# Splitting the first weight unit by k-tile, and moving two later splits of a unit, in a two-layer transformer kernel on one core

## The chip, the core and the metric

The kernel runs on one core of a Trainium2 chip. The metric is the time on the device in microseconds (us) of one execution. Engines are named as in the profile: PE multiplies matrices, PEld loads its stationary operands, ACT is the scalar engine, DVE the vector engine, POOL the GpSimd engine, and SP only issues transfers (DMAs). Each runs its own list of instructions in order and waits on semaphores.

## The reference

Two layers over 256 tokens of 1024 features, all in float32. Layer 0 is NSA attention (16 heads, 4 key/value heads; a compressed, a selected and a window branch, gated), layer 1 is MoBA attention. Behind each attention come a residual with layer norm, a SwiGLU network of width 2816, and again a residual with layer norm.

```python
for i in range(DEPTH):                       # DEPTH = 2
    a = nsa_mixer(x, ...) if i % 2 == 0 else moba_mixer(x, ...)
    x = layer_norm(ALPHA * x + a, ln1_g[i], ln1_b[i])
    f = (jax.nn.silu(x @ wg) * (x @ wu)) @ wd
    x = layer_norm(ALPHA * x + f, ln2_g[i], ln2_b[i])
```

With 256 tokens both attentions see every block, so what is left is causal attention, plus the compressed branch in layer 0.

## The kernel before, in words

**Products.** Each float32 operand is kept as two fp32r parts, hi (rounded by ACT, `copy`, L418) and lo (the rest, subtracted by DVE, `minus`, L685). One float32 product is three matmuls: hi by hi, lo by hi, hi by lo (L1036 to L1038). The 256 tokens are two halves of 128 rows.

**Units.** All weights stream from HBM as 96 units of 128 x 2048 floats (1 MB), each four k-tiles of 128 x 512. Units go round three buffers `raw` and four buffers `w_hi`, `w_lo`. SP loads unit u + 3 when the rest of unit u is taken (`lo_ready`); ACT rounds unit u when it has landed and PE has finished unit u - 4 (`w_used`, in `round_unit`); DVE subtracts (`rest_of_unit`); PE multiplies (`one_unit`, `rows_by_weights`): for each token half four k-tiles of three matmuls, 24 in all. `round_to(n)` on ACT and `rest_to(n)` on DVE do all units below n that are not yet done; where these calls stand in ACT's and DVE's lists is written by hand.

**Opening.** x (transposed) comes in four quarters of 256 KB: for each token half, k-tiles 0 to 3 and 4 to 7, in the order (half 0, first), (half 1, first), (half 0, second), (half 1, second). Units 0 and 1 come in the pieces of `PIECES`: unit 0 as k-tiles 0, 1, and 2 with 3; unit 1 as two pairs. ACT's queue loads the first two pieces, SP's queue the rest and x. ACT rounds and DVE subtracts in the order x0, piece 0, x1, piece 1, piece 2, x2, piece 3, x3, piece 4. PE first runs 25 products of a constant tile (`WARM_UP`, 256 columns, bf16, their result is not used) and then takes each piece for both token halves.

**NSA attention.** Sixteen jobs of two heads each. PE: scores of job i + 2, turn the probabilities of job i, weigh the values of job i - 1 (L1214, L1229, L1247). DVE: `row_maxima(i + 2)`, `scale_probs(i + 1)`. ACT: exp(i + 2). Unit 11, used by PE after job 14, is subtracted by DVE in four quarters, `rest_of_quarter`, in jobs 1 to 4.

**Chunk end.** A SwiGLU network is eleven chunks of 256 hidden features; c = 10 is the last. PE turns the hidden rows (L1313), ACT rounds them (`hidden_hi`, tile last_hi), DVE subtracts (`hidden_lo`, last_lo), PE makes the last down products, and DVE adds the residual (L915), takes the statistics (L920) and writes x (L942), which PE turns (L1071) for the next layer. In the first network unit 48 (the second of layer 1) is rounded whole behind last_hi and subtracted whole behind last_lo.

Of the kernel before, what the change touches and what calls it, by code (L numbers as in the profile page):

```python
# [26 lines left out]
HALF = 2  # L27
# [32 lines left out]
def build(nc, x_rows, x_cols, stream, w_gates, w1, w2, cpos, positions, norms, out):  # L60
# [8 lines left out]
    with ExitStack() as ctx:  # L69
# [84 lines left out]
        piece_in = [sem(f"piece_in{n}") for n in range(3)]  # L154
# [102 lines left out]
        PIECES = (((0, 1), (1, 2), (2, 4)), ((0, 2), (2, 4)))  # L257
# [4 lines left out]
        def open_piece(u, n):  # L262

            return 2 * u + n
# [39 lines left out]
        def _(sp):  # L304
# [9 lines left out]
            load_x(0)  # L314
            load_x(1)
            load_piece(0, 2)
            load_x(2)
            load_piece(1, 0)
            load_x(3)
            load_piece(1, 1)  # L320
# [93 lines left out]
        def _(act):  # L414
# [11 lines left out]

            def round_to(end):
                for u in range(units[0], end):
                    round_unit(u)
                units[0] = max(units[0], end)  # L430
# [36 lines left out]
            part_hi(0, 0)  # L467
            x_hi(1)
            part_hi(0, 1)
            part_hi(0, 2)  # L470
            x_hi(2)
            part_hi(1, 0)
            x_hi(3)
            part_hi(1, 1)
# [118 lines left out]
            def ffn(u0, c0):  # L593
# [36 lines left out]
                silu_of(c, u0 + 3 * c + 1)  # L630
                hidden_hi(c, last_hi)
                round_to(min(UNITS, u0 + 3 * c + 5))
# [36 lines left out]
        def _(dve):  # L669
# [21 lines left out]
            def rest_of_quarter(u, n):  # L691
                at = slice(512 * n, 512 * (n + 1))
                if n == 0:
                    dve.wait_ge(hi_ready, u + 1)
                ins = minus(w_lo[:, u % SLOTS, at], raw[:, u % RAW, at], w_hi[:, u % SLOTS, at].bitcast(f32))
                if n == 3:
# [45 lines left out]
            part_lo(0, 0)  # L742
            x_lo(1)
            part_lo(0, 1)
            part_lo(0, 2)
            x_lo(2)
            part_lo(1, 0)
            x_lo(3)
            part_lo(1, 1)
# [97 lines left out]
            def attend(jobs, job, j0, a0, u):  # L847
# [33 lines left out]
                row_maxima(0)  # L881
                row_maxima(1)
                scale_probs(0)
                scale_probs(1)
                if j0 > 0:
                    rest_to(u + 2)
                for i in range(jobs):
# [4 lines left out]
                    if j0 == 0 and 1 <= i <= 4:  # L892
                        rest_of_quarter(u + 1, i - 1)
# [77 lines left out]
            def ffn(u0, c0):  # L971
# [36 lines left out]
                hidden(c)  # L1008
                hidden_lo(c, last_hi, last_lo)
                rest_to(min(UNITS, u0 + 3 * c + 5))  # L1010
# [22 lines left out]
        def _(pe):  # L1033
# [82 lines left out]
            for _ in range(WARM_UP):  # L1116
                nc.tensor.matmul(ps[:, 7, 0:256], warm_in[:, 0:P], warm_in[:, :], start=True, stop=True)
            for u in range(2):
                for n, (k0, k1) in enumerate(PIECES[u]):
                    if last_piece(u, n):  # L1120
                        pe.wait_ge(lo_ready, u + 1)
                    else:
# [368 lines left out]
```

## Time and profile before

| | us |
|---|---|
| median of 3 runs | 659.43 (659.05 to 659.87) |
| profiled execution | 659.21 |
| its span, first to last instruction | 657.5 |
| PE busy | 641.8 (98%) |
| PEld busy | 512.7 (78%) |
| DVE busy | 399.8 (61%) |
| ACT busy | 313.1 (48%) |
| DMA traffic | 113.03 MB, mean 172 GB/s |

The span is shorter than the time by 1.7 us, which lie around the program. Busy times overlap; an engine's busy time counts for the end only where the others wait for it. A matmul's row is longer than its share of PE's time, since the next one starts before it has drained: the distance from start to start is the cost. The same holds in part for ACT and DVE.

### The profile page before, as it was taken

How to read it: one execution, taken by the hardware profiler on the slowest of the kernel's cores; microseconds unless marked ns; L12 is line 12 of the kernel's file. 1: busy time of each engine (PE TensorE's matmuls, PEld its weight loads, DVE VectorE, ACT ScalarE, POOL GpSimd, SP SyncE). 2: the span in 40 equal slices, each digit the busy share in tenths (PEclk: the TensorE clock that was granted, in tenths of full speed). 3: DMA queues.
4: the chain of work that ended last, by engine and by line, in shares of the span. 5: the costliest groups of instructions: out<-in, count | busy, mean ns of one | idle time of the engine just before them, and what ended most of it. 6: DMA issues, size and time to landing. Idle time of an engine off the chain costs nothing.

```text
span 657.5 us, 8484 instructions
## 1 busy us (share of the span) xinstructions
PE 641.8 (98%) x3265; PEld 512.7 (78%) x3265; DVE 399.8 (61%) x506; ACT 313.1 (48%) x438; POOL 16.3 (2%) x56
## 2 busy tenths in 40 slices
PE   7999999999999999999999999999999999999995
PEld 5887766677888888888867887778788888888874
DVE  4694679868565554444467755786675555544437
ACT  4664578935453444444433645793353344444420
POOL 2000000000000000000000000000100000000001
PEclk8999999999999999999999999999999999999999
DMA  8984311035574555555542654303656555555301
GB/s 299 360 334 183 129 65 65 2 129 191 169 285 187 191 193 191 191 189 179 183 151 94 250 177 173 140 29 125 232 199 253 189 190 191 191 191 191 128 1 64
DMA packets 18574, 113.03 MB, mean 172 GB/s; under 512 B 2800, under 2 KB 3312, under 8 KB 5872
## 3 DMA queue, kind: packets, MB, share of 16 engines
q1 hardware_dynamic: 16384, 102.65, 42.9%
q10 hardware_dynamic: 1008, 5.77, 2.3%
q0 software_dynamic: 1152, 4.19, 1.9%
q8 instruction: 21, 0.34, 0.2%
q14 instruction: 9, 0.07, 0.0%
HBM read 111.56 MB, written 1.05 MB: 171 GB/s over the span
## 4 chain that ended last, share of the span: by engine, by line
PE 86%; DVE 10%; ACT 2%; DMA 1%; issue 1%; DVEq 0%; SPq 0%; ACTq 0%
PE ps L1036 25%; PE ps L1038 24%; PE ps L1037 24%; PE ps L1214 2%; DVE w_lo L685 2%; PE ps L1247 2%; PE ps L1313 2%; PE ps L1229 1%; DVE bn L920 1%; DVE x L934 1%; DVE x L915 1%; PE ps L1155 1%; DMA twice<-x_cols 1%; DVE arena L869 1%; PE ps L1218 1%; ACT w_hi L418 1%
## 5 line engine op out<-in xcount | busy, mean ns | idle before, releaser
L685 DVE TENSOR_TENSOR w_lo<-raw,w_hi 128x2048 fp32r<-128x2048 f32 (+2 forms) x102 | 220.4, 2165 | 102.2 <-ACT w_hi L418 101.8
L1036 PE MATMUL ps<-w_hi,a_hi 128*128 128x512 f32 x592 | 235.8, 398 | 2.3 <-DVE a_lo L685 1.5
L1038 PE MATMUL ps<-w_hi,a_lo 128*128 128x512 f32 x592 | 231.4, 391 | 0.0
L1037 PE MATMUL ps<-w_lo,a_hi 128*128 128x512 f32 x592 | 231.1, 390 | 0.0
L418 ACT ACTIVATE w_hi<-raw 128x2048 fp32r<-128x2048 f32 (+2 forms) x99 | 184.2, 1863 | 96.6 <-PE ps L1038 88.7
L1036 PEld LDWEIGHTS ps<-w_hi,a_hi 128*128 128x128 f32 x592 | 111.6, 188 | 26.7 <-DVE a_lo L685 2.0
L1038 PEld LDWEIGHTS ps<-w_hi,a_lo 128*128 128x128 f32 x592 | 111.4, 188 | 24.0
L1037 PEld LDWEIGHTS ps<-w_lo,a_hi 128*128 128x128 f32 x592 | 111.7, 189 | 21.9
L1036 PE MATMUL ps<-w_hi,h_hi 128*128 128x512 f32 x160 | 62.4, 390 | 0.0
L1038 PE MATMUL ps<-w_hi,h_lo 128*128 128x512 f32 x160 | 62.3, 390 | 0.0
L1037 PE MATMUL ps<-w_lo,h_hi 128*128 128x512 f32 x160 | 62.2, 389 | 0.0
L597 ACT ACTIVATE arena<-ps 128x512 f32<-128x512 f32 x18 | 10.8, 598 | 68.4 <-PE ps L1038 68.4
L418 ACT ACTIVATE h_hi<-ps 128x512 fp32r<-128x512 f32 x20 | 12.0, 599 | 60.2 <-PE ps L1313 60.2
L551 ACT ACTIVATE arena<-ps,neg_max 128x128 f32<-128x128 f32 (+1 forms) x96 | 39.4, 446 | 2.3 <-DVE neg_max L853 2.3
L974 DVE TENSOR_TENSOR arena<-arena,ps 128x512 f32<-128x512 f32 x18 | 12.4, 688 | 37.9 <-ACT arena L597 37.9
L1038 PEld LDWEIGHTS ps<-w_hi,h_lo 128*128 128x128 f32 x160 | 30.0, 188 | 6.3
L1037 PEld LDWEIGHTS ps<-w_lo,h_hi 128*128 128x128 f32 x160 | 30.0, 188 | 6.2
L1036 PEld LDWEIGHTS ps<-w_hi,h_hi 128*128 128x128 f32 x160 | 30.0, 188 | 6.2
L418 ACT ACTIVATE arena<-ps 128x768 f32<-128x768 f32 (+2 forms) x28 | 23.5, 843 | 22.0 <-PE ps L1038 12.0
L685 DVE TENSOR_TENSOR h_lo<-ps,h_hi 128x512 fp32r<-128x512 f32 x20 | 13.8, 690 | 28.5 <-ACT h_hi L418 28.5
L853 DVE TENSOR_REDUCE neg_max<-ps 128x2 f32<-128x256 f32 (+1 forms) x48 | 24.4, 551 | 8.8 <-PE ps L1218 8.2
L418 ACT ACTIVATE a_hi<-ps 128x256 fp32r<-128x256 f32 (+1 forms) x28 | 13.7, 498 | 20.9 <-PE ps L1071 19.0
(150 smaller groups left out, 471.6 us busy)
## 6 DMA issues: line engine op xcount, KB each, us to landing
raw<-stream SPq DMA_DIRECT2D x94, 1024.0 KB, 4.8
arena<-w ACTq DMA_DIRECT2D x4, 1024.0 KB, 13.4
rows<-norms POOLq DMA_DIRECT2D x8, 512.0 KB, 4.6
raw<-stream SPq DMA_DIRECT2D x3, 512.0 KB, 9.1
twice<-x_cols SPq DMA_DIRECT2D x4, 256.0 KB, 7.6
x<-x_rows ACTq DMA_DIRECT2D x1, 1024.0 KB, 4.8
out<-x SPq DMA_DIRECT2D x3, 256.0 KB, 2.1
raw<-stream ACTq DMA_DIRECT2D x2, 256.0 KB, 5.9
```

Of the source, the lines that this page charges most:

```text
L418: return nc.scalar.activation(dst, src, ACT.Copy, scale=scale)
L551: last = nc.scalar.activation(probs[:, b, at:at + keys], ps[:, s_bank(b, h), P * half:P * half + keys], ACT.Exp, bias=neg_max[:, j0 + i, h ...
L597: nc.scalar.activation(silu[:, :, :], ps[:, 0:2, 0:FC], ACT.Silu).then_inc(silu_ready, 1)
L685: return nc.vector.tensor_tensor(dst, a, b, ALU.subtract)
L853: last = nc.vector.tensor_reduce(neg_max[:, j0 + i, half, :], ps[:, s_bank(b, 0):s_bank(b, 1) + 1, P * half:P * half + keys], AX.X, ALU.ma ...
L974: nc.vector.tensor_tensor(h_rows[:, :, :], silu[:, :, :], ps[:, 0:2, FC:2 * FC], ALU.mult).then_inc(h_ready, 1)
L1036: nc.tensor.matmul(dst, hi, m_hi, start=start, stop=False)
L1037: nc.tensor.matmul(dst, hi, m_lo, start=False, stop=False)
L1038: return nc.tensor.matmul(dst, lo, m_hi, start=False, stop=stop)
L1214: nc.tensor.matmul(ps[:, s_bank(b, h), P * half:P * half + keys], qT[on, q, P * half:P * (half + 1)], kk[on, k, 0:keys], start=half == 0, ...
L1247: nc.tensor.matmul(dst[HD * h:HD * (h + 1)], values[:, 0, cols[h]:cols[h] + HD], probsT[:, b, S * h:S * (h + 1)], start=j0 > 0, stop=False)
L1313: last = nc.tensor.transpose(hT_ps[:, half, t, :], h_rows[:, half, P * t:P * (t + 1)], ident[:, :])
```

## The change

The first unit now comes in four pieces of one k-tile (all 256 KB), and pieces 2 and 3 go ahead of the second x quarter, in SP's queue and in ACT's and DVE's order; unit 1's second piece goes ahead of the last x quarter. PE takes both units half by half: all pieces for token half 0, then for half 1, and between the pieces of unit 0's first half it runs four constant products each time (`BETWEEN`, twelve in all). In the NSA attention `rest_of_quarter` goes, and unit 11 is subtracted whole between `row_maxima(0)` and `row_maxima(1)`. At the end of the first network unit 48 is rounded and subtracted in two halves of 1024 columns, the first before last_hi and last_lo, the second behind them; the second network's end has no further unit and stays.

```diff
--- before.py
+++ after.py
@@ -151,7 +151,7 @@
         lo_ready = sem("lo_ready")
         w_used = sem("w_used")
         xT_in = [sem(f"xT_in{q}") for q in range(4)]
-        piece_in = [sem(f"piece_in{n}") for n in range(3)]
+        piece_in = [sem(f"piece_in{n}") for n in range(4)]
         piece_hi = sem("piece_hi")
         piece_lo = sem("piece_lo")
         warm_in_ready = sem("warm_in_ready")
@@ -254,14 +254,15 @@
 
         TURN_BANK = [(4, 5, 6, 7), (0, 1, 4, 5)] * 2
 
-        PIECES = (((0, 1), (1, 2), (2, 4)), ((0, 2), (2, 4)))
+        PIECES = (((0, 1), (1, 2), (2, 3), (3, 4)), ((0, 2), (2, 4)))
+        BETWEEN = 4
         WARM_UP = 25
 
         OUT_PIECES = ((0, 0, 512), (0, 512, 1024), (1, 0, 512), (1, 512, 768), (1, 768, 1024))
 
         def open_piece(u, n):
 
-            return 2 * u + n
+            return 3 * u + n
 
         def last_piece(u, n):
             return n == len(PIECES[u]) - 1
@@ -312,12 +313,13 @@
                 sp.dma_start(raw[:, u, at], stream[u, :, at]).then_inc(landed, 16)
 
             load_x(0)
+            load_piece(0, 2)
+            load_piece(0, 3)
             load_x(1)
-            load_piece(0, 2)
             load_x(2)
             load_piece(1, 0)
+            load_piece(1, 1)
             load_x(3)
-            load_piece(1, 1)
             sp.dma_start(raw[:, 2, :], stream[2]).then_inc(raw_in[2], 16)
             sp.dma_start(pos_i[:, :], positions).then_inc(small_in, 16)
             sp.dma_start(wg_raw[:, :, :], w_gates).then_inc(small_in, 16)
@@ -424,6 +426,15 @@
                     act.wait_ge(w_used, TURN_UNITS * later + (u - SLOTS + 1))
                 copy(w_hi[:, u % SLOTS, :], raw[:, u % RAW, :]).then_inc(hi_ready, 1)
 
+            def round_half_unit(u, part):
+                at = slice(1024 * part, 1024 * (part + 1))
+                if part == 0:
+                    act.wait_ge(raw_in[u % RAW], 16 * (u // RAW + 1))
+                    act.wait_ge(w_used, u - SLOTS + 1)
+                copy(w_hi[:, u % SLOTS, at], raw[:, u % RAW, at]).then_inc(piece_hi if part == 0 else hi_ready, 1)
+                if part == 1:
+                    units[0] = u + 1
+
             def round_to(end):
                 for u in range(units[0], end):
                     round_unit(u)
@@ -464,14 +475,13 @@
                 copy(w_hi[:, u, at], raw[:, u, at]).then_inc(hi_ready if last_piece(u, n) else piece_hi, 1)
 
             x_hi(0)
-            part_hi(0, 0)
+            for n in range(4):
+                part_hi(0, n)
             x_hi(1)
-            part_hi(0, 1)
-            part_hi(0, 2)
             x_hi(2)
             part_hi(1, 0)
+            part_hi(1, 1)
             x_hi(3)
-            part_hi(1, 1)
             units[0] = 2
             round_to(4)
             act.wait_ge(angles_ready, 1)
@@ -628,8 +638,11 @@
                 c = NFC - 1
                 round_to(min(UNITS, u0 + 3 * c + 4))
                 silu_of(c, u0 + 3 * c + 1)
+                if u0 < U_FF1:
+                    round_half_unit(u0 + 3 * c + 4, 0)
                 hidden_hi(c, last_hi)
-                round_to(min(UNITS, u0 + 3 * c + 5))
+                if u0 < U_FF1:
+                    round_half_unit(u0 + 3 * c + 4, 1)
 
             def nsa_values():
                 act.wait_ge(w_used, U_WO0)
@@ -688,12 +701,14 @@
                 dve.wait_ge(hi_ready, TURN_UNITS * later + (u + 1))
                 minus(w_lo[:, u % SLOTS, :], raw[:, u % RAW, :], w_hi[:, u % SLOTS, :].bitcast(f32)).then_inc(lo_ready, 1)
 
-            def rest_of_quarter(u, n):
-                at = slice(512 * n, 512 * (n + 1))
-                if n == 0:
+            def rest_of_half_unit(u, part, done):
+                at = slice(1024 * part, 1024 * (part + 1))
+                if part == 0:
+                    dve.wait_ge(piece_hi, 4 + done)
+                else:
                     dve.wait_ge(hi_ready, u + 1)
                 ins = minus(w_lo[:, u % SLOTS, at], raw[:, u % RAW, at], w_hi[:, u % SLOTS, at].bitcast(f32))
-                if n == 3:
+                if part == 1:
                     ins.then_inc(lo_ready, 1)
                     units[0] = u + 1
 
@@ -739,14 +754,13 @@
 
             nc.vector.memset(warm_in[:, :], 1.0).then_inc(warm_in_ready, 1)
             x_lo(0)
-            part_lo(0, 0)
+            for n in range(4):
+                part_lo(0, n)
             x_lo(1)
-            part_lo(0, 1)
-            part_lo(0, 2)
             x_lo(2)
             part_lo(1, 0)
+            part_lo(1, 1)
             x_lo(3)
-            part_lo(1, 1)
             units[0] = 2
             rest_to(3)
 
@@ -879,18 +893,17 @@
                     minus(a_lo[:, :, t, :], out_ps(t), a_hi[:, :, t, :].bitcast(f32)).then_inc(a_lo_ready, 1)
 
                 row_maxima(0)
+                if j0 == 0:
+                    rest_to(u + 2)
                 row_maxima(1)
                 scale_probs(0)
                 scale_probs(1)
-                if j0 > 0:
-                    rest_to(u + 2)
+                rest_to(u + 2)
                 for i in range(jobs):
                     if i + 2 < jobs:
                         row_maxima(i + 2)
                     if 0 < i and i + 1 < jobs:
                         scale_probs(i + 1)
-                    if j0 == 0 and 1 <= i <= 4:
-                        rest_of_quarter(u + 1, i - 1)
                     if i >= 2 and job(i - 2)[4]:
                         outputs_lo(i - 2)
                     if i >= jobs - 2:
@@ -1006,8 +1019,11 @@
                 c = NFC - 1
                 rest_to(min(UNITS, u0 + 3 * c + 4))
                 hidden(c)
+                if u0 < U_FF1:
+                    rest_of_half_unit(u0 + 3 * c + 4, 0, 1)
                 hidden_lo(c, last_hi, last_lo)
-                rest_to(min(UNITS, u0 + 3 * c + 5))
+                if u0 < U_FF1:
+                    rest_of_half_unit(u0 + 3 * c + 4, 1, 1)
 
             attend(**NSA)
             norm(0, U_FF0, A_O0)
@@ -1113,16 +1129,23 @@
 
 
             pe.wait_ge(warm_in_ready, 1)
-            for _ in range(WARM_UP):
-                nc.tensor.matmul(ps[:, 7, 0:256], warm_in[:, 0:P], warm_in[:, :], start=True, stop=True)
+            def constant_products(count):
+                for _ in range(count):
+                    nc.tensor.matmul(ps[:, 7, 0:256], warm_in[:, 0:P], warm_in[:, :], start=True, stop=True)
+
+            constant_products(WARM_UP)
             for u in range(2):
-                for n, (k0, k1) in enumerate(PIECES[u]):
-                    if last_piece(u, n):
-                        pe.wait_ge(lo_ready, u + 1)
-                    else:
-                        pe.wait_ge(piece_lo, open_piece(u, n) + 1)
-                    for half in range(HALF):
-                        pe.wait_ge(a_lo_ready, 2 * u + half + 1)
+                for half in range(HALF):
+                    for n, (k0, k1) in enumerate(PIECES[u]):
+                        if half == 0:
+                            if u == 0 and n > 0:
+                                constant_products(BETWEEN)
+                            if last_piece(u, n):
+                                pe.wait_ge(lo_ready, u + 1)
+                            else:
+                                pe.wait_ge(piece_lo, open_piece(u, n) + 1)
+                        if n == 0:
+                            pe.wait_ge(a_lo_ready, 2 * u + half + 1)
                         last = rows_by_weights(u, u, half, half, tiles=range(k0, k1))
                 last.then_inc(w_used, 1)
             chunk(2, (2, 3))
```

## Rows read from the trace of the kernel before

**Rows 1.** The page, chain that ended last: share of the span by engine.

```profile
PE 86%; DVE 10%; ACT 2%; DMA 1%; issue 1%; DVEq 0%; SPq 0%; ACTq 0%
```

**Rows 2.** Timeline of PE, 0 to 34 us: start us, us, what, [idle before <-releaser].

```profile
1.27 5.07 PE L1117 MATMUL ps<-warm_in 128*128 128x256 bf16 x25 [1.27 <-DVE warm_in L740]
7.00 0.50 PE L1036 MATMUL ps<-w_hi,a_hi 128*128 128x512 f32 x1 [0.66 <-DVE w_lo L685]
...
9.49 0.80 PE L1036 MATMUL ps<-w_hi,a_hi 128*128 128x512 f32 x1 [1.53 <-DVE a_lo L685]
...
12.62 0.39 PE L1037 MATMUL ps<-w_lo,a_hi 128*128 128x512 f32 x1
...
21.28 0.39 PE L1036 MATMUL ps<-w_hi,a_hi 128*128 128x512 f32 x1
```

**Rows 3.** Stretches: length, busy PE PEld DVE ACT POOL (starts), PEclk, DMA share, GB/s.

```profile
5.80:9.20 3.40, 1.51 (x8) 0.72 (x6) 1.59 (x3) 1.44 (x3) 0.00 (x0) 1.00 0.96 327
9.20:12.60 3.40, 3.11 (x7) 2.49 (x8) 2.41 (x4) 2.37 (x4) 0.00 (x0) 0.50 1.03 420
21.30:82.50 61.20, 61.20 (x363) 48.87 (x361) 41.13 (x59) 35.83 (x35) 1.25 (x2) 1.00 0.64 242
340.00:343.40 3.40, 2.04 (x10) 1.35 (x8) 3.19 (x7) 1.92 (x1) 1.00 (x1) 1.00 0.69 284
```

**Rows 4.** Timeline of ACT, 0 to 34 us.

```profile
8.73 0.63 ACT L418 ACTIVATE w_hi<-raw 128x512 fp32r<-128x512 f32 x1
...
11.97 1.06 ACT L418 ACTIVATE w_hi<-raw 128x1024 fp32r<-128x1024 f32 x1 [0.41 <-DMA raw<-stream]
...
16.44 1.92 ACT L418 ACTIVATE w_hi<-raw 128x2048 fp32r<-128x2048 f32 x1 [1.50 <-DMA raw<-stream]
```

**Rows 5.** Timeline of DVE, 0 to 34 us.

```profile
13.06 1.23 DVE L685 TENSOR_TENSOR w_lo<-raw,w_hi 128x1024 fp32r<-128x1024 f32 x1 [0.16 <-ACT w_hi L418]
```

**Rows 6.** DMA issues, 1.7 to 2.2 us (ACT's second piece): KB, us to landing.

```profile
raw<-stream ACTq DMA_DIRECT2D x1, 256.0 KB, 7.4
```

**Rows 7.** Timeline of DVE, 68 to 108 us.

```profile
85.88 1.02 DVE L853 TENSOR_REDUCE neg_max<-ps 128x2 f32<-128x256 f32 x2 [2.17 <-PE ps L1218]
...
94.25 0.68 DVE L685 TENSOR_TENSOR w_lo<-raw,w_hi 128x512 fp32r<-128x512 f32 x1
```

**Rows 8.** Timeline of PE, 86 to 118 us.

```profile
92.89 0.93 PE L1214 MATMUL ps<-kk,qT 64*128 64x128 f32 x8 [0.40 <-ACT arena L551]
...
94.39 0.66 PE L1229 MATMUL ps<-ident,arena 128*128 128x128 f32 x4 [0.25 <-DVE arena L869]
...
105.46 0.93 PE L1214 MATMUL ps<-kk,qT 64*128 64x128 f32 x8
...
106.54 0.60 PE L1229 MATMUL ps<-ident,arena 128*128 128x128 f32 x4
...
117.00 0.93 PE L1214 MATMUL ps<-kk,qT 64*128 64x128 f32 x8
```

**Rows 9.** Timeline of DVE, 322 to 362 us.

```profile
332.13 0.69 DVE L974 TENSOR_TENSOR arena<-arena,ps 128x512 f32<-128x512 f32 x1 [1.77 <-ACT arena L597]
334.20 0.69 DVE L685 TENSOR_TENSOR last_lo<-ps,last_hi 128x512 fp32r<-128x512 f32 x1 [1.38 <-ACT last_hi L418]
336.00 2.29 DVE L685 TENSOR_TENSOR w_lo<-raw,w_hi 128x2048 fp32r<-128x2048 f32 x1 [1.11 <-ACT w_hi L418]
...
342.79 1.41 DVE L942 SCALAR_TENSOR_TENSOR x<-x,rstd,rows 128x512 f32<-128x512 f32 x2
```

**Rows 10.** Timeline of PE, 322 to 362 us.

```profile
334.95 0.50 PE L1036 MATMUL ps<-w_hi,last_hi 128*128 128x512 f32 x1
...
343.60 1.32 PE L1071 MATMUL ps<-ident,x 128*128 128x128 f32 x8 [1.55 <-DVE x L942]
```

**Rows 11.** Timeline of DVE, 638 to 652 us.

```profile
647.47 1.41 DVE L942 SCALAR_TENSOR_TENSOR x<-x,rstd,rows 128x512 f32<-128x512 f32 x2
```

**Rows 12.** Timeline of PE, 638 to 652 us.

```profile
641.11 0.50 PE L1036 MATMUL ps<-w_hi,last_hi 128*128 128x512 f32 x1
```

## The prediction

> **What bounds the kernel now.** I read the chain of waits on the page first [rows 1]: 86% of it is PE, 10% DVE. So PE's queue of products sets the time, and only the places count where PE stands, or where its clock is low. Next came PE's own waits and its time in stretches. From 21.3 to 82.5 us PE is busy for all of 61.20 us [rows 3]; a shift of the work before passes through this stretch whole, whether it is a gain or a loss. The three places that the change touches are places where PE does not run full.
>
> 1. The opening. Twenty-five constant products run first, three real ones start at 7.00, the fourth at 9.49 after 1.53 us of standing for the second token part; from 9.49 on PE is dense [rows 2]. But the granted clock is 0.50 (1.2 GHz) from 9.2 to 12.6, after a stretch with 1.51 of 3.40 us busy [rows 3]. Seven products take 9.49 to 12.62, 0.45 us each; the 38 after them take 12.62 to 21.28, 0.228 each. At 21.28 unit 2 begins.
> 2. The first half of the NSA attention (jobs 2 to 6), where DVE's turn is longer than PE's.
> 3. The end of the first feed-forward network, where PE stands 1.55 us at 343.60 for x [rows 10].
>
> **The change part by part.**
>
> *Opening, the arrival of the pieces.* The queues carry the same bytes. Unit 0's half of 512 KB becomes two of 256 KB, and both are moved ahead of the second x quarter on SP's queue. That is one DMA more on SP (about 0.45 us of issue), with unit 2 and the six small loads behind it. The second piece (k-tile 1) was issued by ACT at about 1.3 and took 7.4 us, so it landed at 8.7 [rows 6]; ACT rounded it at 8.73 [rows 4]. Before, PE did not need it at 9.49: it went on with the same k-tile for the other token half. Now it is the next thing needed: ACT to 9.35, DVE 0.68 us, PE at 10.07. That is 0.58 us later than 9.49. The pieces behind it follow at ACT's 0.6 us, so DVE ends them at 10.65 and 11.2, and x quarter 1 at 11.85. Unit 1's first piece was rounded before x quarter 3 and stays at 14.2 (the 1024 form starts at 13.06 and gives way at 14.20 [rows 5]); its second piece is now before x quarter 3 and ends near 15.4, the quarter at 16.2, early enough for the last twelve products.
>
> *Opening, PE's sum.* From 10.07 there are 45 products, as before from 9.49, and eight constant products among them (the first four of the twelve lie in the standing time). A constant product took 0.20 us on average (25 in 5.07) [rows 2]; it has half the columns of a real one, so at the full clock I take 0.11. With the clock high the whole time: 10.07 + 45 x 0.228 + 8 x 0.11 = 21.2. Unit 2 cannot start before its rest is there: it lands at 16.44, then 1.92 of ACT and 2.29 of DVE make 20.7 [rows 4, 9]; that bound is not the later one. So unit 2 starts at 21.2 instead of 21.28: a gain of 0.1 us, with 0.6 as the most. If the constant products cost 0.20 each, it is a loss of 0.6. If the clock falls at 9.2 and rises at 12.6 as before, 2.5 us run at half pace, which costs 1.25 us more: a loss of 1.15. I take the gain of 0.1, because constant products now stand behind the first piece, but this is the weakest step.
>
> For this the Trainium skill has a sentence (TensorE: Matmul & The Clock Gate, Part 1): the same kernel can show a different count of slow products from run to run, because the points at which the gate is set don't follow the kernel's start. One profile cannot test it. By it, the opening's term would wander between the two values above from run to run, and the median would lie between them.
>
> The trace shows both sides of the clock question: 1.51 of 3.40 us busy was followed by the low clock, while 2.04 of 3.40 us at 340.0 to 343.4 was not [rows 3]. The four constant products behind the first piece bring the first figure to about 2.1 (0.11 x 4 and a tail of 0.17), like the second, though the second has dense work before it.
>
> *Cutting finer.* DVE takes 0.68 us for 512 columns and gives way to the next after 0.60; for 1024 it is 1.23 and 1.14 [rows 5, 7]. So an added cut costs 0.06 us of DVE. That is beside other work in the opening, where PE does not wait for DVE after 10.07, and the quarters that go from the attention were four at 0.60.
>
> The Trainium skill (VectorE: DVE Perf Modes, the errata section) says that an instruction that reads SBUF pays a fixed latency of its own, exposed between instructions, and gives (N + 151)/0.96 ns for a tensor_tensor. The durations agree (0.69 and 1.22 by it), the distance between starts doesn't: by the page four quarters would cost 2.76 us and their removal up to 0.36 more, where the row shows 2.4.
>
> *Unit 11 in the attention.* Removed: four quarter subtractions, 0.60 of pitch each, in jobs 1 to 4. Added: one whole subtraction (2.29, pitch 2.19) between the first two row maxima. DVE stands 2.17 us there, until 85.88, for the scores of job 1 [rows 7]; the whole unit runs 83.63 to 85.82 in that gap, so its cost is nothing with 0.05 to spare, and were the cover gone, the full 2.2 would shift exp(1) and job 2. What goes? PE starts the scores of job 4 at 92.89 and those of job 8 at 105.46: 12.57 us. The next four jobs, where PE is never late, take to 117.00: 11.54 [rows 8]. The excess is 1.03. Of it, 0.42 lies at 94.39, 1.50 after the scores began where 106.54 is 1.08 after 105.46; that turn waits for job 2's scaled probabilities, which no quarter preceded, and it stays. The quarters sit before the other late turns. With them gone DVE needs about 2.4 us a job against PE's 2.88, and PE bounds. Gain 0.6; bounds 0 and 1.0.
>
> *The unit at the chunk end.* Before, ACT rounds it whole after last_hi and DVE subtracts it from 336.00 to 338.2 [rows 9]; only then does DVE add the first quarter of the residual, although PE's first six last products were done by about 336.6 (334.95 and six at 0.228, with their tail). The second network's end has no such unit and is the pattern: first last product 641.11, first x written at 647.47, 6.36 us [rows 11, 12]. Here it is 334.95 to 342.79, 7.84 us [rows 9, 10]. So 1.48 us is the unit's price. Now the first half goes between silu and last_hi: ACT 332.05 to 333.1 (1.06 for 1024 [rows 4]); last_hi started at about 333.6 by DVE's row (0.6 before 334.18), so ACT is free in time. DVE waits for that half behind its product for h_rows, subtracts from 333.14 to 334.28, and last_lo, queued behind it, starts at 334.28 instead of 334.20 [rows 9]. PE waits for last_lo, so 0.08 is lost (0.2 at most). The second half runs 335.15 to 336.3, before PE's sums. Net 1.40. PE was free for the turn at 342.05 (343.60 less 1.55 [rows 10]), 342.1 now, and will start it at 342.2; what is late next is still x, by 0.1. What follows until the second half's turn is ACT and DVE work that starts from this turn (the chain of waits runs through it without PE's products), so the gain stays. Bounds 1.0 and 1.5.
>
> **Sum.** 0.1 + 0.6 + 1.4 = 2.1 us. Against the profiled execution, 659.21 (span 657.5 and 1.7 around it), that is 657.1; that execution is 0.22 under the median of the runs, 659.43, so for the median I say 657.3.
>
> **The rivals.**
> - A, the clock falls anyway. The gap before the second piece is now 1.5 us even behind the constant products (8.6 to 10.07), as long as the one that went before the low clock. Then the opening loses 1.15 and the whole is 659.43 + 1.15 - 2.0 = 658.6. For it: the low stretch that is in the trace [rows 3]. Against it: more work ahead of the gap.
> - B, slower than before. PE's late start at 10.07 and eight constant products at low pace leave the low clock in place for long. Each us at low clock costs 0.5. From 10.07 on, the 2.1 us of the sum are used up when the clock rises only at 14.3 (4.2 us at half pace), and at 16.9 it is 1.3 us slower than before. If it rises at 19.4, 4.6 are lost and the time is 662.0. [...] Against it: the opening of before rose after 3.1 us of dense work, and no low stretch in its work was longer.
> - C, the attention gives nothing: the whole unit overruns its 2.17 us gap, or ACT's exponentials are the next bound behind DVE. For it: the gap is only just long enough [rows 7]. Against it: from 105.46 on the same ACT work keeps up with PE's 2.88 a job [rows 8]. Time 657.9.
> - D, the first half unit holds last_hi or last_lo back by more than the 0.08, and PE's last products with it, by up to 0.9: the chunk end gives 0.5. Against it: ACT has 0.5 us to spare. Time 658.2.
>
> **How the numbers follow.** Forecast 0.5, A 0.28, B 0.06 (of which 0.04 beyond 0.2%), C 0.1, D 0.06. The measurement can tell about 0.2%, 1.3 us: faster means below 658.1, slower above 660.75. Faster holds the forecast, C and half of D and a part of A where the low stretch is short: 0.66. Same 0.30, slower 0.04. The range reaches from 656.3 (all bounds good: 0.6, 1.0, 1.5) to 659.1, which takes in A with a costly constant product; the forecast's own range is 656.6 to 658.0.
>
> **What would show it.** In the changed trace: PE's second real group near 10.07, not 9.49; granted clock 1.00 through 9.2 to 12.6 (or 0.50 for A); unit 2's first product at 21.2. A whole 2048 subtraction ending just before the second row maxima, which start within 0.1 us of PE's scores, and 11.9 to 12.0 us between the scores of jobs 4 and 8. First last product to first x 6.4 us at the end of the first network, with last_lo 0.1 later relative to h_rows, and PE's stand before the turn at 0.1 to 0.2. The prediction is wrong in its main step if the distance from unit 2's start to the end has not shrunk by 2.0 us.

## The result, and the profile after

The kernel after takes 655.63 us (median of 6 runs, 655.48 to 655.75), the kernel before 659.20 in the same session (6 runs, 659.04 to 659.87): a ratio of 0.9943, 95% interval 0.9933 to 0.9953. That is 3.6 us, where I predicted 2.1, and below my range. The profiled execution took 655.48 with a span of 653.7, 3.8 less than the span of before.

The page of the kernel after, chain that ended last (before: [rows 1]):

```profile
PE 89%; DVE 9%; ACT 2%; issue 0%; DVEq 0%; ACTq 0%
```

DMA has left the chain, DVE has lost a point. Where the time went is read from the distance to before at fixed marks. The first is unit 2's first product, timeline of PE, 0 to 22 us (before: [rows 2]):

```profile
1.27 5.52 PE L1134 MATMUL ps<-warm_in 128*128 128x256 bf16 x25 [1.27 <-DVE warm_in L755]
6.56 0.64 PE L1052 MATMUL ps<-w_hi,a_hi 128*128 128x512 f32 x1
...
7.51 0.61 PE L1134 MATMUL ps<-warm_in 128*128 128x256 bf16 x4
7.88 0.49 PE L1052 MATMUL ps<-w_hi,a_hi 128*128 128x512 f32 x1
...
9.05 0.48 PE L1052 MATMUL ps<-w_hi,a_hi 128*128 128x512 f32 x1
...
10.21 0.48 PE L1052 MATMUL ps<-w_hi,a_hi 128*128 128x512 f32 x1
...
18.94 0.39 PE L1054 MATMUL ps<-w_hi,a_lo 128*128 128x512 f32 x1
19.16 0.40 PE L1052 MATMUL ps<-w_hi,a_hi 128*128 128x512 f32 x1
```

The second group starts at 7.88, not at 10.07, and PE shows no idle from there on. Unit 2 begins at 19.16 against 21.28: 2.12 us. The first two stretches of [rows 3] again, now in the kernel after, same columns:

```profile
5.80:9.20 3.40, 3.40 (x20) 2.31 (x19) 2.79 (x6) 2.48 (x5) 0.00 (x0) 1.00 0.85 304
9.20:12.60 3.40, 3.40 (x19) 2.62 (x19) 2.40 (x3) 2.56 (x4) 0.00 (x0) 1.00 1.04 417
```

PE is busy for all of both, and the granted clock stays 1.00 (2.4 GHz) where before it was 0.50 (1.2 GHz). ACT's timeline shows that the data came sooner (before: [rows 4]):

```profile
6.10 1.68 ACT L420 ACTIVATE w_hi<-raw 128x512 fp32r<-128x512 f32 x3 [0.40 <-DMA raw<-stream]
8.35 1.32 ACT L420 ACTIVATE a_hi<-twice 128x512 fp32r<-128x512 f32 x2 [0.57 <-DMA twice<-x_cols]
...
14.77 1.92 ACT L420 ACTIVATE w_hi<-raw 128x2048 fp32r<-128x2048 f32 x1 [1.62 <-DMA raw<-stream]
```

The second piece landed at 6.10, where it was 8.73; unit 2 at 14.77, where it was 16.44. DVE's row for unit 2 ends at 19.01, which is when the unit is ready; PE starts it 0.15 later, without a wait, so PE's own products and the unit's readiness end almost together:

```profile
16.72 2.29 DVE L698 TENSOR_TENSOR w_lo<-raw,w_hi 128x2048 fp32r<-128x2048 f32 x1 [2.23 <-ACT w_hi L420]
```

The rate in half microseconds says when the bytes were gained. Before:

```profile
4.50:5.00 0.50, 0.50 (x4) 0.38 (x3) 0.00 (x0) 0.01 (x1) 0.19 (x1) 1.00 1.04 315
5.00:5.50 0.50, 0.50 (x4) 0.33 (x3) 0.00 (x0) 0.50 (x1) 0.00 (x0) 1.00 1.02 168
5.50:6.00 0.50, 0.50 (x6) 0.40 (x4) 0.35 (x1) 0.50 (x2) 0.00 (x0) 1.00 0.80 102
6.00:6.50 0.50, 0.34 (x4) 0.06 (x1) 0.50 (x2) 0.14 (x1) 0.00 (x0) 1.00 0.78 193
```

After:

```profile
4.50:5.00 0.50, 0.50 (x4) 0.38 (x3) 0.00 (x0) 0.45 (x1) 0.19 (x1) 1.00 1.02 397
5.00:5.50 0.50, 0.50 (x4) 0.33 (x3) 0.28 (x1) 0.50 (x2) 0.00 (x0) 1.00 1.06 402
5.50:6.00 0.50, 0.50 (x5) 0.36 (x3) 0.50 (x2) 0.20 (x1) 0.00 (x0) 1.00 1.03 381
6.00:6.50 0.50, 0.50 (x4) 0.24 (x2) 0.50 (x1) 0.40 (x1) 0.00 (x0) 1.00 0.91 320
```

The last figure, GB/s, falls to 102 before and is 320 or more in these slices after, with the DMA engines busy in both (the share ahead of it). The bytes were slow before, not absent: these four slices moved 0.39 MB before, 0.75 after. The prediction used none of these rows.

The attention, DVE and then PE (before: [rows 7, 8]):

```profile
80.63 1.02 DVE L867 TENSOR_REDUCE neg_max<-ps 128x2 f32<-128x256 f32 x2
81.57 2.28 DVE L698 TENSOR_TENSOR w_lo<-raw,w_hi 128x2048 fp32r<-128x2048 f32 x1
83.83 1.02 DVE L867 TENSOR_REDUCE neg_max<-ps 128x2 f32<-128x256 f32 x2
```

```profile
90.84 0.93 PE L1237 MATMUL ps<-kk,qT 64*128 64x128 f32 x8 [0.40 <-ACT arena L561]
...
92.34 0.66 PE L1252 MATMUL ps<-ident,arena 128*128 128x128 f32 x4 [0.25 <-DVE arena L883]
...
102.79 0.93 PE L1237 MATMUL ps<-kk,qT 64*128 64x128 f32 x8
```

The whole unit fills the gap, the second maxima follow without a stand, and from the scores of job 4 to those of job 8 it is 11.95 us instead of 12.57: 0.62.

The chunk end, DVE and then PE (before: [rows 9, 10]):

```profile
329.46 0.69 DVE L987 TENSOR_TENSOR arena<-arena,ps 128x512 f32<-128x512 f32 x1 [1.77 <-ACT arena L607]
330.40 1.23 DVE L698 TENSOR_TENSOR w_lo<-raw,w_hi 128x1024 fp32r<-128x1024 f32 x1 [0.26 <-ACT w_hi L420]
331.55 0.68 DVE L698 TENSOR_TENSOR last_lo<-ps,last_hi 128x512 fp32r<-128x512 f32 x1
332.47 1.23 DVE L698 TENSOR_TENSOR w_lo<-raw,w_hi 128x1024 fp32r<-128x1024 f32 x1 [0.24 <-ACT w_hi L420]
334.07 0.69 DVE L928 SCALAR_TENSOR_TENSOR x<-x,ps 128x512 f32<-128x512 f32 x1 [0.37 <-PE ps L1054]
...
338.66 1.42 DVE L955 SCALAR_TENSOR_TENSOR x<-x,rstd,rows 128x512 f32<-128x512 f32 x2
```

```profile
332.29 0.51 PE L1052 MATMUL ps<-w_hi,last_hi 128*128 128x512 f32 x1
...
339.47 1.32 PE L1087 MATMUL ps<-ident,x 128*128 128x128 f32 x8
```

First last product to first x is 6.37 us (before 7.84, second network 6.36), and from DVE's product for the hidden rows (its first row above, 332.13 before) to PE's turn of x, 11.47 has become 10.01: 1.46. The distance to before is now 4.13. It holds until the third norm, where 0.4 is given back. DVE, then PE:

```profile
462.96 1.41 DVE L947 SCALAR_TENSOR_TENSOR x<-x,mean_var,rows 128x512 f32<-128x512 f32 x2
464.82 1.42 DVE L955 SCALAR_TENSOR_TENSOR x<-x,rstd,rows 128x512 f32<-128x512 f32 x2 [0.46 <-DVE x L947]
```

```profile
465.63 1.32 PE L1087 MATMUL ps<-ident,x 128*128 128x128 f32 x8 [0.74 <-DVE x L955]
```

Before, that turn stood at 469.37 after 0.40 of waiting: 3.74 earlier now. DVE stands 0.46 us ahead of the second row, where it stood for nothing before. It needs the reciprocal root from POOL, which starts 0.08 behind the variance and takes 0.99 in both kernels (to 468.21 and to 464.11); DVE's row begins 0.36 after its end in before (468.57), 0.71 after it here. POOL's rows are rough. The stand of 0.46 is in the profiles of the kernel after, of its second measurement (11) and of runs 5, 6, 7 and 13, and in no other: not in the three parts alone (1 to 3), and not in runs 9 and 10 either, which hold all three parts. So neither a part by itself nor the earlier time makes it; what does stays open.

### The profile page after: what moved, and what is told of

The parts are those of the page before. It is cut to its first block, busy times and chain, and to the rows that moved or that the text cites. A ratio compares the mean times of both kernels' runs of the same rounds, so it can differ in the third digit from the quotient of the medians.

```text
span 653.7 us, 8507 instructions
## 1 busy us (share of the span) xinstructions
PE 641.7 (98%) x3277; PEld 512.8 (78%) x3277; DVE 400.3 (61%) x505; ACT 313.3 (48%) x440; POOL 16.3 (3%) x56
## 4 chain that ended last, share of the span: by engine, by line
PE 89%; DVE 9%; ACT 2%; issue 0%; DVEq 0%; ACTq 0%
PE ps L1052 25%; PE ps L1054 24%; PE ps L1053 24%; PE ps L1237 3%; DVE w_lo L698 2%; PE ps L1270 2%; PE ps L1252 2%; PE ps L1336 2%; DVE bn L933 1%; DVE x L947 1%; DVE x L928 1%; PE ps L1178 1%; PE ps L1134 1%; PE ps L1241 1%; DVE x L955 1%; PE ps L1119 1%
## 5 line engine op out<-in xcount | busy, mean ns | idle before, releaser
L607 ACT ACTIVATE arena<-ps 128x512 f32<-128x512 f32 x18 | 10.8, 599 | 68.3 <-PE ps L1054 68.3
```

## The experiments

Every time is a median beside 15 to 31 runs of before in the same session (medians 659.1 to 659.23). Ratios are to these, with 95% intervals in brackets. Edits are shortened where they show `...`.

**1. The opening alone** (the kernel after with the attention and the chunk end as before).

```diff
                 row_maxima(0)
-                if j0 == 0:
-                    rest_to(u + 2)
                 row_maxima(1)
...
-                if u0 < U_FF1:
-                    round_half_unit(u0 + 3 * c + 4, 0)
                 hidden_hi(c, last_hi)
-                if u0 < U_FF1:
-                    round_half_unit(u0 + 3 * c + 4, 1)
+                round_to(min(UNITS, u0 + 3 * c + 5))
...
```

> The changed opening alone; attention and chunk end as before. Theory (the whole gain is the sum of three separate ones, 2.1 + 0.6 + 1.4, less 0.3 lost later): 2.1 us under before, unit 2's first product near 19.2, unit 2 landed near 14.8, granted clock 1.00 through 9 to 12.6. Rival (the opening gives the predicted 0.1 and the rest is interplay of the parts): 0.1 under before, unit 2 at 21.2.

657.32 (657.25 to 657.70, 8 runs), ratio 0.9974 [0.9964, 0.9984]: 1.8 us. Unit 2 landed at 14.87, its first product came at 19.22.

**2. The attention alone.**

```diff
                 row_maxima(0)
+                if j0 == 0:
+                    rest_to(u + 2)
                 row_maxima(1)
...
-                    if j0 == 0 and 1 <= i <= 4:
-                        rest_of_quarter(u + 1, i - 1)
```

> Unit 11 subtracted whole between the first two row maxima, nothing else changed. Theory: 0.6 us under before; 11.95 us between the scores of jobs 4 and 8 instead of 12.57. Rival (the gap only exists in step with the changed opening): no gain, second row maxima late.

658.55 (658.08 to 660.15, 11 runs), 0.9994 [0.9985, 1.0003]. The time does not tell it from nothing; the trace does: job 4 to job 8 takes 11.95, from 93.48 to 105.43.

**3. The chunk end alone.**

```diff
+                if u0 < U_FF1:
+                    round_half_unit(u0 + 3 * c + 4, 0)
                 hidden_hi(c, last_hi)
-                round_to(min(UNITS, u0 + 3 * c + 5))
+                if u0 < U_FF1:
+                    round_half_unit(u0 + 3 * c + 4, 1)
...
```

> The unit at the chunk end in two halves, nothing else changed. Theory: 1.4 us under before at the end of the first network; 6.4 us from the first last product to the first x. Part of it may be lost later where PE waits for POOL's root in the third norm (0.3). Rival: the gain is given back in the second layer, under 0.5.

657.61 (657.45 to 658.35, 10 runs), 0.998 [0.997, 0.9989]: 1.5 us. The three alone give 1.8 + 0.55 + 1.5 = 3.85 against 3.6 together; the loss at the third norm, which is in none of the three, has the size of the difference. So two parts are as predicted and the opening holds the miss.

**4. Before, with the second x quarter behind unit 0** in SP's queue, nothing else.

```diff
             load_x(0)
-            load_x(1)
             load_piece(0, 2)
+            load_x(1)
```

> The kernel before with one swap in SP's queue: unit 0's second half is issued ahead of x quarter 1, all engines' orders unchanged. Theory order (the slow transfers at 5 to 7.5 us come from x quarter 1 going beside the first pieces): the dip moves or shrinks, piece 1 lands by about 6.5 instead of 8.7 and unit 2 near 15 instead of 16.4; the time is within 1 us of before, since PE still needs x quarter 1 for its fourth product. Rival chance (the dip is a state of that execution): the same dip at 5 to 6.5 us, unit 2 at 16.4.

659.61 (657.88 to 661.01, 10 runs), 1.0009 [1.0, 1.0018]. The rate holds, and unit 2 landed at 14.80, as in the kernel after:

```profile
4.50:5.00 0.50, 0.50 (x7) 0.44 (x6) 0.00 (x0) 0.00 (x0) 0.19 (x1) 1.00 1.10 422
5.00:5.50 0.50, 0.50 (x6) 0.27 (x3) 0.00 (x0) 0.27 (x1) 0.00 (x0) 1.00 1.05 373
5.50:6.00 0.50, 0.08 (x1) 0.00 (x0) 0.11 (x1) 0.50 (x2) 0.00 (x0) 1.00 0.96 348
```

Yet the median doesn't gain. PE still takes each piece for both token halves, and ACT and DVE still take the second x quarter ahead of the second piece. The quarter lands at 8.09 as before, and PE stands 1.30 us for it (before 1.53). The times then go with the mean granted clock: 0.997 in the fastest run (657.88), 0.990 and 0.991 in the two slowest (660.30, 661.01). The profiled run is the fastest: its clock stays at 1.00, unit 2 is ready at 19.04, and PE gets to it only at 19.93. The landing alone is not the gain; PE has to be able to use it.

**5. After, with the second x quarter back in second place.**

```diff
             load_x(0)
+            load_x(1)
             load_piece(0, 2)
             load_piece(0, 3)
-            load_x(1)
```

> The changed kernel with x quarter 1 put back to second place in SP's queue, all engines' orders as changed. Theory order: the slow stretch at 5 to 7.5 us is back, piece 1 lands near 8.7, unit 2 near 16.4, unit 2's first product at 21 or later: 657.3 to 658, that is 1.7 us or more over the changed kernel. Rival: the finer cut of unit 0 made the landing early; 655.6.

657.14 (656.94 to 659.32, 8 runs), 0.9976 [0.9965, 0.9986]: 1.5 us of the gain are gone. The low rate is back, the second piece lands at 7.98 and unit 2 at 16.54, and unit 2's first product comes at 20.83:

```profile
4.50:5.00 0.50, 0.50 (x4) 0.38 (x3) 0.00 (x0) 0.27 (x1) 0.19 (x1) 1.00 0.87 164
5.00:5.50 0.50, 0.50 (x4) 0.32 (x3) 0.10 (x1) 0.50 (x2) 0.00 (x0) 1.00 0.97 172
5.50:6.00 0.50, 0.50 (x4) 0.37 (x3) 0.50 (x1) 0.38 (x1) 0.00 (x0) 1.00 0.88 139
...
16.54 1.92 ACT L420 ACTIVATE w_hi<-raw 128x2048 fp32r<-128x2048 f32 x1 [1.59 <-DMA raw<-stream]
```

**6. After without the twelve constant products** between the pieces.

```diff
-        BETWEEN = 4
+        BETWEEN = 0
```

> The changed kernel without its twelve constant products between the pieces. Theory clock (they are there to hold the granted clock, and cost nothing since unit 2 bounds): PE stands up to 0.4 us between the pieces, the clock falls in some executions at 9 to 11, the times spread over 1 us or more and the median is 0.3 to 1.5 us above the changed kernel's 655.6. Rival (with pieces arriving every 0.6 us the products alone hold the clock): 655.6 with the same small spread, or less.

655.60 (655.47 to 656.16, 4 runs), 0.995 [0.9933, 0.9966]: the same as with them. PE is done with its products earlier and waits for unit 2:

```profile
19.15 0.50 PE L1052 MATMUL ps<-w_hi,a_hi 128*128 128x512 f32 x1 [0.66 <-DVE w_lo L698]
```

**7. After without the constants, and PE's order of before** (each piece for both halves).

```diff
             for u in range(2):
-                for half in range(HALF):
-                    for n, (k0, k1) in enumerate(PIECES[u]):
...
+                for n, (k0, k1) in enumerate(PIECES[u]):
...
+                    for half in range(HALF):
+                        pe.wait_ge(a_lo_ready, 2 * u + half + 1)
```

> The changed kernel with PE's order of before (each piece for both token halves) and without constant products; queues and the orders of ACT and DVE as changed. Theory order of work (token half 0 first lets PE use the pieces while x quarter 1 is under way): PE stands from 7.8 to about 9.7 for x quarter 1 and the clock then depends on the execution: 656.0 to 658, a spread of 1 us or more. Rival (unit 2's arrival bounds, PE's order is free): 655.6, small spread.

658.04 (656.39 to 659.60, 10 runs), 0.9984 [0.9971, 0.9996], 2.4 us over run 6 by the medians. The time goes with the mean clock, from 0.996 (656.39) to 0.992 (659.60). PE stands 2.06 us for the second x quarter, and then the products are at the low clock for a time:

```profile
7.28 0.40 PE L1054 MATMUL ps<-w_hi,a_lo 128*128 128x512 f32 x1
9.73 0.51 PE L1052 MATMUL ps<-w_hi,a_hi 128*128 128x512 f32 x1 [2.06 <-DVE a_lo L698]
...
11.60 0.63 PE L1052 MATMUL ps<-w_hi,a_hi 128*128 128x512 f32 x1
...
14.66 0.40 PE L1054 MATMUL ps<-w_hi,a_lo 128*128 128x512 f32 x1
```

**8. Before, with four constant products** between the first piece's two token halves.

```diff
                     for half in range(HALF):
+                        if u == 0 and n == 0 and half == 1:
+                            for _ in range(4):
+                                nc.tensor.matmul(ps[:, 7, 0:256], warm_in[:, 0:P], warm_in[:, :], ...)
```

> The kernel before with four constant products between the first piece's two token halves, where PE stands 1.5 us. Theory clock by idle time (they hold the clock): the low clock in the products is gone in most executions, spread under 0.5 us, 658.6, the fastest of before's runs. Rival (they are too short to matter): 659.1 and before's spread of 1.2.

658.95 (658.81 to 659.24, 10 runs), 0.9996 [0.9987, 1.0006]. No run's mean clock is under 0.996; the spread is 0.43 us over 10 runs, where before has 2.14 over 31 (658.63 to 660.77, mean clock 0.997 to 0.991). The clock stays high in the two stretches where it fell in before; this kernel, then before:

```profile
9.00:12.00 3.00, 2.29 (x9) 1.61 (x9) 2.05 (x3) 2.06 (x3) 0.00 (x0) 1.00 1.04 421
12.00:15.00 3.00, 2.55 (x12) 2.06 (x12) 2.85 (x4) 2.58 (x3) 0.00 (x0) 1.00 1.04 397
```

```profile
9.00:12.00 3.00, 2.51 (x6) 2.03 (x7) 2.01 (x3) 1.97 (x4) 0.00 (x0) 0.53 1.05 425
12.00:15.00 3.00, 3.00 (x13) 2.40 (x13) 2.75 (x5) 2.61 (x3) 0.00 (x0) 0.90 1.05 397
```

But unit 2 lands at 16.54, is ready at 20.78 (before 20.68) and begins at 20.84: with the clock mended, no more than this can be had while the landing stays.

**9. After, with unit 0's last two k-tiles in one piece of 512 KB.**

```diff
-        PIECES = (((0, 1), (1, 2), (2, 3), (3, 4)), ((0, 2), (2, 4)))
+        PIECES = (((0, 1), (1, 2), (2, 4)), ((0, 2), (2, 4)))
...
```

> The changed kernel with unit 0's last two k-tiles as one piece of 512 KB again (three pieces), everything else as changed. Theory: the finer cut is worth nothing, since unit 2's readiness bounds: 655.6. Rival (the cut lets PE work dense and holds the clock): 655.9 to 657.

656.36 (655.94 to 656.38, 4 runs), 0.9957 [0.9941, 0.9972]. By the medians the fine cut is worth about 0.8 (beside 655.57 for the kernel after, run 11). The second piece landed at 7.50 and unit 2's first product came at 20.05, 0.83 later than in run 11, though the unit itself landed at 14.92 and was ready at 19.15: here PE is late, not unit 2.

**10 and 11. Unit 2 rounded and subtracted in two halves**, and `BETWEEN = 0` (no constant products between the pieces), and the kernel after once more beside it.

```diff
+            act.wait_ge(raw_in[2], 16)
+            copy(w_hi[:, 2, 0:1024], raw[:, 2, 0:1024]).then_inc(piece_hi, 1)
+            copy(w_hi[:, 2, 1024:2048], raw[:, 2, 1024:2048]).then_inc(hi_ready, 1)
-            units[0] = 2
+            units[0] = 3
...
+            dve.wait_ge(piece_hi, 5)
+            minus(w_lo[:, 2, 0:1024], ...)
+            dve.wait_ge(hi_ready, 3)
+            minus(w_lo[:, 2, 1024:2048], ...).then_inc(lo_ready, 1)
...
```

> The changed kernel without constant products, and unit 2 rounded and subtracted in two halves of 1024 columns. Theory (unit 2's readiness at 19.0 bounds the opening, its landing at 14.8 and two whole passes of 1.92 and 2.29 make it): the halves overlap, unit 2 is ready at 18.1, PE is done with units 0 and 1 at about 18.1, so 0.9 us under the changed kernel: 654.8. Rival (without constants and with less slack the clock falls in some executions, or unit 3 is next): 655.3 to 656 with a wide spread.

> The changed kernel itself on this chip, as the base for the others of this call: 655.6 and a spread under 0.4 us.

654.50 (654.21 to 654.67, 5 runs), 0.9929 [0.9915, 0.9942], beside 655.57 (655.49 to 655.68, 5 runs), 0.9945 [0.9932, 0.9959], for the kernel after. That is 1.07 us better, and the best version. DVE and PE with the halves, then PE of the kernel after:

```profile
15.80 2.36 DVE L701 TENSOR_TENSOR w_lo<-raw,w_hi 128x1024 fp32r<-128x1024 f32 x2 [1.35 <-ACT w_hi L420]
...
18.24 0.47 PE L1058 MATMUL ps<-w_hi,a_hi 128*128 128x512 f32 x1
```

```profile
19.22 0.40 PE L1052 MATMUL ps<-w_hi,a_hi 128*128 128x512 f32 x1
```

Unit 2 landed at the same time in both (14.70 and 14.77). Two things differ: the passes from landing to ready are cut in half, and the constant products are gone. The traces say that it needs both. With constants and whole passes PE is busy up to its start at 19.22, while unit 2 is ready at 19.01. Without the constants alone (run 6) PE waits 0.66 for the unit and starts at 19.15. With both, unit 2 is ready at 18.16 and PE starts at 18.24. The halves with the constants were not run; since PE's own products last until 19.22 with them, little could have come of it. The start is 0.98 earlier; the rest of the 1.28 between the two profiled executions (654.21 and 655.49) lies at the third norm, where run 10 doesn't have the stand of 0.46.

The Trainium skill (VectorE: DVE Perf Modes, the errata section) gives (N + 151)/0.96 ns for a tensor_tensor of N columns and has each instruction pay the fixed part; an estimate from it is 2.45 us for the two halves. This trace doesn't bear that out: the row has 2.36 for both, against 2.29 for the whole, so the cut costs 0.07.

**12 to 16. What makes the rate fall.** Five kernels change how, from where or by which queue the second x quarter is read.

Before, x stored so that each quarter is one block in memory; then the same on the kernel after:

```diff
-                sp.dma_start(x_quarter(x_cols_raw, q), x_quarter(x_cols, q))
+                sp.dma_start(x_quarter(x_cols_raw, q), x_cols[q, :, :])
...
```

> The kernel before with each x quarter laid out contiguously in HBM (256 KB in a row, 2 KB to a partition) instead of 2 KB pieces at a pitch of 8 KB. Theory layout (x's quarters are slow to read because of their pitch beside a second stream with the same pitch): the slow stretch shrinks, x quarter 1 lands before 7, unit 2 near 15. Rival (it is the pair of transfers in flight, wherever they lie): the dip stays at 5 to 7.5 us and unit 2 lands at 16.4, 659.1.

> The changed kernel with the same contiguous x. Theory layout: the dip at 6.5 to 7.5 us goes too, unit 2 lands 0.3 us earlier, 655.3. Rival: 655.6.

658.21 (657.72 to 658.75, 10 runs), 0.9983 [0.9974, 0.9993], and 655.92 (655.79 to 656.15, 4 runs), 0.9951 [0.9934, 0.9968]. The low rate comes earlier instead of going (143 and 139 GB/s in the slices from 4.0 to 5.0 in the first), the first quarter lands late (6.24 against 4.99 in before, 5.48 against 4.55 in the kernel after), and unit 2 lands at 15.84 and 14.80.

Before, with 64 columns of padding in each row of x:

```diff
+                lo = KT * P * half + 512 * part
-                sp.dma_start(x_quarter(x_cols_raw, q), x_quarter(x_cols, q))
+                sp.dma_start(x_quarter(x_cols_raw, q), x_cols[:, lo:lo + 512])
...
```

> The kernel before with the rows of x's array 8448 bytes apart instead of 8192. Theory pitch (the streams hit the same places of HBM because all pitches are 8192 bytes): the dip shrinks or goes, unit 2 lands near 15, 658 or less. Rival: dip and time as before, 659.1.

659.06 (657.68 to 660.29, 10 runs), 0.9996 [0.9986, 1.0005]. Again the low rate moved (156 and 143 GB/s at 3.5 to 4.5, 348 at 5.0 to 5.5), and unit 2 lands at 15.98.

Before, the second quarter read from unit 3's first k-tile. The second token half is then computed from these weights instead of x, so only the transfers and the time mean something:

```diff
+                src = stream[3, :, 0:512] if q == 1 else x_quarter(x_cols, q)
-                sp.dma_start(x_quarter(x_cols_raw, q), x_quarter(x_cols, q))
+                sp.dma_start(x_quarter(x_cols_raw, q), src)
```

> The kernel before, but x quarter 1 is read from unit 3's first k-tile of the weight stream (so the second token half is computed from wrong data; the size, place in the queue and destination are the same). Theory source (x's own array is slow to read): the dip at 5 to 7.5 us goes, unit 2 lands near 15. Rival (place in the queue: two short transfers started together beside each other, whatever their source): the dip stays, 16.4.

658.22 (657.95 to 658.56, 10 runs), 0.9987 [0.9977, 0.9997]. The quarter landed at 6.90 and unit 2 at 15.66, with a shallower fall at 4.5 to 5.5 (270 and 315 GB/s) and another at 3.0 to 3.5 (143). But the layout and the padding, which read the same array, brought unit 2 to 15.84 and 15.98 and moved as many bytes: from 2.0 to 7.5 the mean is 266 GB/s here, 260 and 263 there, 237 in before, and the time with the quarters in blocks is the same (658.21). So it is not shown that the array matters.

Before, the first two pieces issued by SP too, so that one queue carries all:

```diff
             load_x(0)
+            sp.dma_start(raw[:, 0, 0:512], stream[0, :, 0:512]).then_inc(piece_in[0], 16)
             load_x(1)
+            sp.dma_start(raw[:, 0, 512:1024], stream[0, :, 512:1024]).then_inc(piece_in[1], 16)
             load_piece(0, 2)
...
```

> The kernel before with the first two weight pieces issued by SP between x quarters 0 and 1 instead of by ACT (order x0, piece 0, x1, piece 1, rest). Theory two queues (the slow stretch needs the two queues' short transfers side by side): no dip at 5 to 7.5, unit 2 near 15. Rival (x quarter 1's early place alone makes it): dip as before. Two more issues of 0.45 us on SP move unit 2's issue to about 6.

658.77 (658.15 to 659.80, 10 runs), 0.9996 [0.9987, 1.0005]. The fall stays (238, 111, 135 GB/s at 4.5 to 6.0, and 235 as the mean from 2.0 to 7.5), so two queues side by side are not its cause.

## Why the prediction was wrong

**The step that failed** is "Opening, the arrival of the pieces": "The second piece (k-tile 1) was issued by ACT at about 1.3 and took 7.4 us, so it landed at 8.7." I took the landings of before as fixed, and only moved what stood behind them. They belonged to the order of the queue. The 7.4 us [rows 6] were long because the second x quarter was being read beside that piece at a fallen rate. With the quarter behind the pieces, the piece landed at 6.10. The error went on into "PE's sum" twice: the second group's 10.07, which was 7.88, and the bound "it lands at 16.44, then 1.92 of ACT and 2.29 of DVE make 20.7", which made 0.6 the most that I would grant. The unit landed at 14.77 and was ready at 19.01 (14.77 to the end of DVE's row, 16.72 and 2.29). The opening gave 1.8 (alone) to 2.1 (by the trace), not 0.1. Run 5 shows it: the queue order alone is worth 1.5 of it. With landings near those that I took, run 5 starts unit 2 at 20.83, 0.45 sooner than before and within my bound of 0.6, and its time, 657.14, is near my 657.3. The rest of "PE's sum" held: with 7.88 in place of 10.07 it gives 19.0, and 19.16 was measured.

**The constant products.** Their price was right in order: 0.37 between groups for four (7.51 to 7.88), about 0.1 each. Their merit was nil here: run 6 has the same time. I had the clock stay high "because constant products now stand behind the first piece"; in the kernel after it stays high without them, since DVE makes a piece ready every 0.6 us, three products take 0.7, and PE shows no stand between the pieces. They are not free for what comes next: PE with them is busy until unit 2 is ready, and only without them could run 10 start it sooner. In the kernel before, with its hole, they do keep the clock high (run 8). What holds the clock in the kernel after is PE's order, which no longer needs the second x quarter early (run 7).

**Rival A**, the clock falling anyway, left no sign in the 15 runs of the kernel after and of run 6, whose mean granted clock is 0.996 or more. Nor did B. The page that I cited (the Trainium skill, TensorE: Matmul & The Clock Gate, Part 1: the count of slow products changes from run to run) fits the kernel before and runs 4 and 7, whose times spread by 2 to 3 us with the mean clock. The kernel after spreads by 0.3, and neither of its two profiles has a slow product. The count itself hardly differs in the profiles of before's opening (before, runs 2 and 3): seven, eight and eight products at half pace. A dense opening takes away the spread as well as the time.

**The attention** gave 0.62, predicted 0.6, by the mechanism predicted: the quarters were in DVE's way where DVE was the later, and job 2's turn stayed 1.50 us behind the scores (90.84 to 92.34, before 92.89 to 94.39). Rival C fell. **The chunk end** gave 1.46, predicted 1.40: the second network's end was the right pattern (6.36, and 6.37 measured). I had PE wait 0.1 to 0.2 for x at the turn; the row shows no wait. Rival D fell. **The third norm**'s loss of about 0.4 was not in the sum, which let every gain pass through to the end.

By terms: predicted 0.1 + 0.6 + 1.4 = 2.1; measured in the trace 2.1 + 0.6 + 1.5 - 0.4 = 3.8, which is the difference of the spans.

## What stays open

Why the second x quarter is slow to read when it stands second. Not the two queues (16). Layout, padding and source (12 to 15) each lessen or move the fall, by about as much, and none removes it. In the kernel after there is one too, later and where less hangs on it (176 and 160 GB/s at 6.5 to 7.5); that it has the same cause is not shown. Open as well is what makes the stand at the third norm come with some kernels and not with others.

## What to carry to other kernels

A landing time in a profile is not a property of the transfer but of the order in which all were issued: before bounding what an opening can give by a landing, look at the rate in short slices, and if it falls well under what the same queues reach a microsecond later, take the landing as open. Give the first work to do only what has arrived (here one token half of all pieces), and the clock may need no filler, as here (run 6). Then ask what the first full-size unit waits for between landing and use; cutting its two passes in half, with the filler products taken out, gave another 1.1 us.

## What the runs showed of the hardware that was not expected

- The same bytes in another order landed 1.67 us sooner (16.44 against 14.77). The busy share of the DMA engines tells little of the rate: at 5.5 to 6.0 it was 0.80 with 102 GB/s in before and 1.03 with 381 in the kernel after, and at 5.0 to 5.5 it was 1.02 with 168 in before and 1.06 with 402 in the kernel after.
- The low clock came after a stand of only 0.66 and of 1.53 us between products [rows 2] in before, and after 2.06 in run 7. With one and the same opening it began at a different time in each profile: 9.2 in before, 10.2 in run 2, 10.8 in run 3. The length of a stand alone doesn't tell: in run 12 PE stood 2.79 us ahead of its first real product, and the granted clock stayed at 1.00.
- For one kernel the times spread by up to 3 us, with the mean granted clock: run 4 went from 657.88 (0.997) to 661.01 (0.991), run 7 from 656.39 (0.996) to 659.60 (0.992).
